# Gated units' projections as products of rounded high and low parts, with the convolution taps reordered around the gating

## The chip, the cores and the metric

The kernel runs on one core of one Trainium2 chip. The metric is the device time of one execution in microseconds (us). The engines are PE (TensorE: matmuls, with PEld, its weight loads, shown apart), DVE (VectorE), ACT (ScalarE), POOL (GpSimd) and SP (SyncE, which only issues transfers here). Each engine works through its own program in order and waits on semaphores.

## The reference, cut to what matters

One layer of a diffusion backbone works on 1024 latent tokens (a 16 x 64 grid) and 256 context tokens, with 1024 model columns. The part at issue is the first half of the combined projection and what is made of it:

```python
h = rms_norm(x, norm1_g) * (1 + scale1) + shift1
u = h @ w_in                                # 1024 -> 4608 columns
val, gate = u[..., :512], u[..., 512:1024]  # the convolution branch
v = val * sigmoid(gate)                     # the gated units
v = depthwise_conv(v, width=31) + dw_b      # per channel, over tokens
v = silu(layer_norm(v)) @ w_pw
q, k, value = three blocks of 512 columns of u, for the attention
```

Behind it come the neighbourhood attention, the merge of the two branches with its projections, the output projection, a router that picks tokens for 16 experts (SwiGLU, 1024 to 2048 to 1024), and a final RMSNorm. All data are float32, and the change leaves what is computed as it is, up to rounding.

## The kernel before, in words

**Layout.** Activations stand transposed: `hT` holds h as 8 chunks k of 128 channels (partitions) by 1280 tokens. The tokens are worked on in three blocks tc of 512, 512 and 256 (`TOK`). Almost all of SBUF is one float32 tensor `arena`; named regions of it are reused (HT, CONV, GLU, Q, K, V, R). The helpers `mm` (line 658) and `tr` (line 661) record all matmuls and transposes. A matmul whose operands are float32 stands in the trace as two records; one whose operands are of type fp32r (float32 rounded for the array) stands as one.

**Front.** The input rows are squared, scaled by 1/rms (DVE, ACT), transposed on PE, and copied into `hT`. PE also makes the first columns of the modulation vectors (`ada`, `ada_turn`). Then `affine` turns `hT` into h in place: even chunks on ACT (line 1225), odd chunks on DVE (line 1638).

**Gated units** (PE from line 714 with half = 0; ACT line 1235; DVE line 1672). Four units j = 2i + jj, each for 128 value columns and the 128 gate columns that belong to them. SP loads the weights of unit j into `ws[j % 2]` (lines 387 and 388) once unit j - 2 has been multiplied, and the modulation weights (line 393) for two `ada` calls per unit. For each unit and token block PE multiplies 2 banks x 8 chunks (bank `2*tc` the values, `2*tc+1` the gates), each as a plain float32 matmul. ACT takes the sigmoid of the gate bank, DVE multiplies it with the value bank into `glu` (`gated_unit`) and raises `u_free`, which lets PE reuse the two banks. Between them PE does `ada` behind blocks 0 and 1 and `ada_turn` behind blocks 1 and 2, and ACT copies their results (lines 1143 and 1147) right behind the sigmoid of its block; PE's next `ada_turn` waits for that copy.

**Convolution** (DVE, lines 1674 to 1711). For each of 4 channel groups, 31 taps over 1310 columns: tap 0 is a scale and bias (line 1679), the other 30 are multiply-adds `conv = glu * dw + conv` (line 1683), each waiting for the one before it. Their order against the gating is written out by hand: DVE gates a block, then does some taps, then gates the next one. Behind the last tap `conv_done` is raised.

**Queries and keys** (the same PE loop with half = 1). Four more passes of the same shape, plain float32 matmuls into the same banks. ACT empties both banks (lines 1242 and 1243), raises `qk_free`, and makes the modulation copies. Before the first pass PE waits once, for all the gating (`u_free` 15).

**Behind it.** PE sums over channels for the LayerNorm (`channel_sums`, waits for `conv_done`), then come values, attention, the merge, the output projection and the experts. The merge and the experts already multiply in three products: the high part of each operand is its fp32r rounding (ACT Copy), the low part is the rest (DVE subtract, line 1846 for h, 1800 for weights), and PE does high x high, high x low and low x high. GpSimd works in the front only on memsets; later it adds attention biases (lines 568 to 578), sums softmax terms, and issues the gathers (line 631) and scatters (lines 639 and 642) of the experts, which read their row numbers from SBUF.

## Time and profile before

| | |
|---|---|
| median of 3 executions | 2777.97 us (2774.75 to 2778.36) |
| the profiled execution | 2777.72 us, span 2775.9 us |
| PE busy | 2656.1 us, 96% of the span |
| DVE, ACT, POOL busy | 1725.9, 1284.0, 192.4 us |
| gated units on PE | 51.4 to about 204 us |
| queries and keys on PE | 205.0 to about 355 us |
| convolution on DVE | 91.9 to 294.8 us |
| attention, merge, output projection, experts | the rest |

The span runs from the first to the last instruction of the core; the time of the execution is 1.8 us longer. All times in the rows are from the span's start. A mean of "one" is the duration of one record; records of matmuls overlap, so the rate of PE is read from where successive weight loads start. "Idle" names the time an engine stood still before an instruction and what ended it.

### The profile page before, as it was taken

Reading aid. Unit: us, or ns where it says so; the run is one execution under the profiler, and the core shown is the slowest. Engines: PE = TensorE matmul, PEld = TensorE weight load, DVE = VectorE, ACT = ScalarE, POOL = GpSimd, SP = SyncE. Lnnn points to the kernel's source line nnn. Section 1 sums busy time; section 2 is a strip of 40 time slices with the busy share of each in tenths; the row PEclk is TensorE's granted clock in tenths of the full one; section 3 lists DMA queues with packets and bytes.
Section 4 is the critical chain, followed back from the end, with each engine's and each line's share of the span. In section 5 each row is a group of like instructions: output and inputs, shape, how many; then the busy total and the mean of one; then the engine's idle time right before and its main releaser. Section 6 shows DMA issues by size and latency. Waiting matters only on the chain.

```text
span 2775.9 us, 49590 instructions
## 1 busy us (share of the span) xinstructions
PE 2656.1 (96%) x21723; PEld 2024.0 (73%) x21723; DVE 1725.9 (62%) x2079; ACT 1284.0 (46%) x1867; POOL 192.4 (7%) x180
## 2 busy tenths in 40 slices
PE   6999999999999999869999999999999999999994
PEld 3555577666777897647887788778777877787783
DVE  4699234766434354556676677767667676776664
ACT  4000034555323232255565556656565555555554
POOL 0000011110000000000110011001101110110000
PEclk9999999999999999979999999999999999999997
DMA  8322222000333372277898889789879888898884
GB/s 260 91 90 78 61 56 50 15 1 25 91 100 98 99 202 110 107 243 268 283 298 258 283 291 287 268 281 293 281 265 298 276 282 274 288 296 259 283 276 169
DMA packets 457504, 543.75 MB, mean 196 GB/s; under 512 B 26304, under 2 KB 409387, under 8 KB 457290
## 3 DMA queue, kind: packets, MB, share of 16 engines
q1 hardware_dynamic: 449610, 519.60, 57.2%
q0 software_dynamic: 7680, 20.98, 3.4%
q8 instruction: 173, 2.83, 0.4%
q14 instruction: 41, 0.34, 0.0%
HBM read 513.27 MB, written 27.28 MB: 195 GB/s over the span
## 4 chain that ended last, share of the span: by engine, by line
PE 90%; DVE 5%; ACT 2%; DMA 1%; issue 1%; SPq 0%; POOL 0%; DVEq 0%; POOLq 0%; ACTq 0%
PE bank L658 85%; PE bank L661 4%; DVE arena L1683 2%; DVE arena L1756 1%; DVE arena L1766 1%; ACT arena L1287 1%; DVE arena L2102 0%; DMA arena<-in_x_sample 0%; ACT arena L1291 0%; DMA arena<-xhat,arena 0%; DMA arena<-in_w_attn_o 0%; DMA arena<-in_w_in 0%; DVE arena L1612 0%; DMA yacc<-arena 0%; DMA arena<-yacc 0%
## 5 line engine op out<-in xcount | busy, mean ns | idle before, releaser
L2032 DVE TENSOR_TENSOR slot_lo<-slot,e_hi 128x2048 fp32r<-128x2048 f32 x256 | 579.4, 2289 | 166.3 <-ACT e_hi L1496 162.6
L658 PE MATMUL bank<-arena 128*64 128x128 f32 (+8 forms) x3492 | 636.1, 396 | 19.0 <-ACT arena L1287 5.1
L658 PEld LDWEIGHTS bank<-arena 128*128 128x128 f32 (+3 forms) x3492 | 388.8, 163 | 238.5 <-issue 170.9
L1496 ACT ACTIVATE e_hi<-slot 128x2048 fp32r<-128x2048 f32 x256 | 481.4, 1917 | 0.0
L658 PE MATMUL bank<-e_hi,xe_hi 128*128 128x512 f32 x1024 | 418.0, 408 | 0.0
L658 PE MATMUL bank<-e_hi,xe_lo 128*128 128x512 f32 x1024 | 404.7, 395 | 0.0
L658 PE MATMUL bank<-slot_lo,xe_hi 128*128 128x512 f32 x1024 | 400.2, 391 | 0.0
L658 PE MATMUL bank<-slot,arena 128*32 128x128 f32 (+1 forms) x10240 | 363.6, 297 | 6.1 <-DVE arena L2042 3.5
L658 PEld LDWEIGHTS bank<-slot,arena 128*32 128x32 f32 x10240 | 285.2, 111 | 72.6 <-issue 34.2
L2036 DVE TENSOR_TENSOR slot_lo<-slot,e_hi 128x2048 fp32r<-128x2048 f32 x128 | 289.0, 2291 | 77.8 <-ACT e_hi L1498 77.8
L661 PE MATMUL bank<-arena 128*128 128x128 f32 (+3 forms) x1415 | 202.6, 275 | 54.9 <-DVE arena L1612 12.3
L1498 ACT ACTIVATE e_hi<-slot 128x2048 fp32r<-128x2048 f32 x128 | 239.4, 1912 | 29.6 <-PE bank L658 29.6
L661 PEld LDWEIGHTS bank<-arena 128*128 128x128 f32 (+3 forms) x1415 | 161.5, 142 | 114.2 <-issue 77.1
L658 PEld LDWEIGHTS bank<-e_hi,xe_hi 128*128 128x128 f32 x1024 | 191.9, 187 | 58.8 <-issue 16.1
L658 PEld LDWEIGHTS bank<-slot_lo,xe_hi 128*128 128x128 f32 x1024 | 192.4, 188 | 47.5
L658 PEld LDWEIGHTS bank<-e_hi,xe_lo 128*128 128x128 f32 x1024 | 192.5, 188 | 37.0
L1518 ACT ACTIVATE arena<-bank 128x256 f32<-128x256 f32 x128 | 49.2, 385 | 359.8 <-PE bank L658 359.8
L658 PE MATMUL bank<-e_hi,hT_hi 128*128 128x512 f32 x512 | 209.4, 409 | 0.0
L658 PE MATMUL bank<-e_hi,hT_lo 128*128 128x512 f32 x512 | 202.3, 395 | 0.0
L658 PE MATMUL bank<-slot_lo,hT_hi 128*128 128x512 f32 x512 | 200.0, 391 | 0.0
L1683 DVE SCALAR_TENSOR_TENSOR arena<-arena 128x1310 f32<-128x1310 f32 x120 | 189.9, 1583 | 4.0
L1800 DVE TENSOR_TENSOR w_down<-arena,w_up 128x2048 fp32r<-128x2048 f32 x23 | 52.7, 2293 | 141.5 <-ACT wx_up L1341 95.9
(231 smaller groups left out, 2878.8 us busy)
## 6 DMA issues: line engine op xcount, KB each, us to landing
slot<-in_w_gate_e SPq DMA_DIRECT2D x128, 1024.0 KB, 5.9
slot<-in_w_up_e SPq DMA_DIRECT2D x128, 1024.0 KB, 9.2
slot<-in_w_down_e SPq DMA_DIRECT2D x128, 1024.0 KB, 6.7
arena<-in_w_in SPq DMA_DIRECT2D x68, 512.0 KB, 5.1
arena<-in_w_ada SPq DMA_DIRECT2D x48, 512.0 KB, 4.8
arena<-in_w_conv_pw SPq DMA_DIRECT2D x24, 256.0 KB, 5.6
arena<-in_w_attn_o SPq DMA_DIRECT2D x24, 256.0 KB, 5.3
yacc<-arena SPq DMA_DIRECT2D x10, 512.0 KB, 2.6
```

What stands on the lines that cost most here:

```text
L658: return nc.tensor.matmul(out, lhsT, rhs, start=start, stop=stop)
L661: return nc.tensor.transpose(out, in_, ident[0:n, 0:n])
L1287: A_(Pctx[g % 2][h][:, 0:n], bank[3 + h][:, 0:n], ACT.Exp, bias=m, accum_out=sums[:, g % 2, h, 1:2]).then_inc(pc_ok, 1)
L1496: A_(halves(e_hi[c % 2])[:, :, rows4, :], halves(slot[q])[:, :, rows4, :], ACT.Copy).then_inc(ehi_ok, 1)
L1498: A_(e_hi[c % 2][:, 8 * h:8 * h + 8, :], slot[q][:, 8 * h:8 * h + 8, :], ACT.Copy).then_inc(ehi_ok, 1)
L1518: A_(sil[:, (c - 1) % 2, :], bank[(c - 1) % 2][:, 0:256], ACT.Silu).then_inc(silu_ok, 1)
L1683: V_.scalar_tensor_tensor(out=conv[:, k, :], in0=glu[:, k, t:t + CONV_W], scalar=dw[:, k, t:t + 1], in1=conv[:, k, :], op0=ALU.mult, op1=A ...
L1756: V_.tensor_reduce(mx[:, g % 2, h, 1:2], bank[3 + h][:, 0:n], AX_X, ALU.max).then_inc(c_max, 1)
L1766: V_.tensor_copy(PT[:, h, o:o + 512], src).then_inc(tg_dve, 1)
L1800: last = V_.tensor_tensor(dst, src[:, 0:16, :], w_up[s].bitcast(F32), ALU.subtract)
L2032: V_.tensor_tensor(halves(slot_lo[q])[:, :, rows4, :], halves(slot[q])[:, :, rows4, :], halves(e_hi[c % 2])[:, :, rows4, :].bitcast(F32), ...
L2036: V_.tensor_tensor(slot_lo[q][:, rows8, :], slot[q][:, rows8, :], e_hi[c % 2][:, rows8, :].bitcast(F32), ALU.subtract).then_inc(elo_ok, 1)
```

## The change

Four things are changed. First, the gated units' matmuls become three fp32r products each: high and low parts of h (`g_up`, `g_down`) and of the unit's weights (`gw_up`, `gw_down`). ACT rounds the high parts (24 pieces of h and 8 half weights); DVE subtracts the low parts of h (24) and of the first unit's weights (2), and GpSimd those of the other three units' weights (6). `g_down` lies where `hT` lies and `gw_down` where `ws` lies, so the plain values are overwritten; `g_up` lies in the regions K and V and `gw_up` in Q, where queries and keys are written later. Second, GpSimd adds the parts of h back into `hT` (24 adds), each block as soon as the last gated unit has multiplied it; PE's first queries wait for each chunk (`pool_sum`), and ACT waits for all 24 before it writes the first query. Third, the one wait for all gating before the queries becomes a wait per token block. Fourth, the taps are dealt out anew. `res9` becomes `pool_sum`, and waits on shared semaphores further on get offsets.

```diff
--- before.py
+++ after.py
@@ -151,6 +151,10 @@
         w_down_first = rounded_at("w_down_first", K, 16, P)
         h_up = [rounded_at(f"h_up{q}", GLU + 1024 * q, 2, 512) for q in range(KD // 2)]
         h_down = [rounded_at(f"h_down{q}", HT + 2 * T * q, 2, T) for q in range(KD // 2)]
+        g_up = [rounded_at(f"g_up{c}", K + T * c, 1, T) for c in range(KD)]
+        g_down = [h_down[c // 2][:, c % 2, :] for c in range(KD)]
+        gw_up = [rounded_at(f"gw_up{i}", Q + 2048 * i, KD, 256) for i in range(2)]
+        gw_down = [rounded_at(f"gw_down{i}", R + 2048 * i, KD, 256) for i in range(2)]
         wo = plain_at("wo_raw", HT, KD, T)[:, :, 0:D]
         wo_conv = rounded_at("wo_conv", CONV, KC, CONV_W)[:, :, 0:D]
         wo_attn = rounded_at("wo_attn", Q, KC, T)[:, :, 0:D]
...
@@ -560,6 +564,19 @@
             nc.gpsimd.memset(eps_zero[0:1, :], 0.0).then_inc(rpb_zero, 1)
             nc.gpsimd.memset(wr, 0.0)
             nc.gpsimd.memset(glu, 0.0).then_inc(pads, 1)
+
+            pool.wait_ge(wl_ok, 2)
+            for j in range(1, 4):
+                for half in range(2):
+                    pool.wait_ge(wh_ok, 2 * j + half + 1)
+                    ks = slice(4 * half, 4 * half + 4)
+                    nc.gpsimd.tensor_tensor(gw_down[j % 2][:, ks, :], ws[j % 2][:, ks, :], gw_up[j % 2][:, ks, :].bitcast(F32),
+                                            ALU.subtract).then_inc(wl_ok, 1)
+            for tc, (t0, n) in enumerate(TOK):
+                pool.wait_ge(u_ready, 18 + 2 * tc + 2)
+                for c in range(KD):
+                    nc.gpsimd.tensor_tensor(hT[:, c, t0:t0 + n], g_up[c][:, 0, t0:t0 + n].bitcast(F32),
+                                            g_down[c][:, t0:t0 + n].bitcast(F32), ALU.add).then_inc(pool_sum, 1)
             pool.wait_ge(conv_done, 1)
             def bias_rows(hp, h):
...
@@ -712,19 +729,29 @@
             for half in range(2):
-                if half:
-                    pe.wait_ge(u_free, 15)
                 for i in range(0, 2):
                     for jj in range(2):
+                        j = 2 * i + jj
                         pe.wait_ge(ws_in[jj], i * 32 + (64 + 64 * half))
                         for tc, (t0, n) in enumerate(TOK):
+                            if half and j == 0:
+                                pe.wait_ge(u_free, 12 + tc + 1)
                             pe.wait_ge(qk_free if half else u_free, i * 6 + (3 * jj + tc + 1))
                             for h in range(2):
+                                out, cols = bank[2 * tc + h][:, 0:n], slice(P * h, P * h + P)
                                 for k in range(KD):
-                                    if half == i == jj == h == 0:
-                                        pe.wait_ge(h_dve if k % 2 else h_act, 4 * tc + k // 2 + 1)
-                                    last = mm(bank[2 * tc + h][:, 0:n], ws[jj][:, k, P * h:P * h + P], hT[:, k, t0:t0 + n],
-                                              k == 0, k == KD - 1)
+                                    if half:
+                                        if j == h == 0:
+                                            pe.wait_ge(pool_sum, 8 * tc + k + 1)
+                                        last = mm(out, ws[jj][:, k, cols], hT[:, k, t0:t0 + n], k == 0, k == KD - 1)
+                                    else:
+                                        if tc == h == 0 and k % 4 == 0:
+                                            pe.wait_ge(wl_ok, 2 * j + k // 4 + 1)
+                                        if j == h == 0:
+                                            pe.wait_ge(hl_ok, 8 * tc + k + 1)
+                                        mm(out, gw_up[jj][:, k, cols], g_up[k][:, 0, t0:t0 + n], k == 0, False)
+                                        mm(out, gw_up[jj][:, k, cols], g_down[k][:, t0:t0 + n], False, False)
+                                        last = mm(out, gw_down[jj][:, k, cols], g_up[k][:, 0, t0:t0 + n], False, k == KD - 1)
                                 last.then_inc(u_ready, 1)
                             if tc:
                                 ada_turn(5 + tc, i * 4 + (8 * half + 2 * jj + tc + 8))
...
@@ -906,8 +933,8 @@
-                        pe.wait_ge(wl_ok, i * 2 + (8 * tc + s + 1))
-                        pe.wait_ge(hl_ok, 12 * tc + 4)
+                        pe.wait_ge(wl_ok, 8 + i * 2 + (8 * tc + s + 1))
+                        pe.wait_ge(hl_ok, 24 + 12 * tc + 4)
...
@@ -1216,14 +1243,44 @@
                         A_(dst[:, c, t0:t0 + n], bank[4 + g % 4][:, 0:n], ACT.Identity, bias=Bc[:, c, cnd:cnd + 1],
                            scale=Ac[:, c, cnd:cnd + 1]).then_inc(done, 1)
             act.wait_ge(t1_act, 12)
-            for g, (c, tc) in enumerate(tile_groups()):
-                if g % 2 == 0:
-                    t0, n = TOK[tc]
-                    cnd = 1 if tc == 2 else 0
-                    if tc == 0:
-                        act.wait_ge(mod1_ok, c // 4 + 1)
-                    A_(hT[:, c, t0:t0 + n], hT[:, c, t0:t0 + n], ACT.Identity, bias=sh1[:, c, cnd:cnd + 1],
-                       scale=A1[:, c, cnd:cnd + 1]).then_inc(h_act, 1)
+            def affine(tc, c):
+
+                t0, n = TOK[tc]
+                cnd = 1 if tc == 2 else 0
+                if tc == 0:
+                    act.wait_ge(mod1_ok, c // 4 + 1)
+                A_(hT[:, c, t0:t0 + n], hT[:, c, t0:t0 + n], ACT.Identity, bias=sh1[:, c, cnd:cnd + 1],
+                   scale=A1[:, c, cnd:cnd + 1]).then_inc(h_act, 1)
+
+            def g_hi(tc, cs_):
+
+                t0, n = TOK[tc]
+                for c in cs_:
+                    act.wait_ge(h_dve if c % 2 else h_act, 4 * tc + c // 2 + 1)
+                    A_(g_up[c][:, 0, t0:t0 + n], hT[:, c, t0:t0 + n], ACT.Copy).then_inc(hh_ok, 1)
+
+            def gw_hi(j, half):
+
+                act.wait_ge(ws_in[j % 2], 64 + 32 * (j // 2))
+                ks = slice(4 * half, 4 * half + 4)
+                A_(gw_up[j % 2][:, ks, :], ws[j % 2][:, ks, :], ACT.Copy).then_inc(wh_ok, 1)
+
+            act.wait_ge(t1_ready, 24)
+            affine(0, 0)
+            affine(0, 2)
+            g_hi(0, range(0, 4))
+            gw_hi(0, 0)
+            affine(0, 4)
+            affine(0, 6)
+            g_hi(0, (4, 5))
+            gw_hi(0, 1)
+            g_hi(0, (6, 7))
+            for tc in (1, 2):
+                for c in range(0, KD, 2):
+                    affine(tc, c)
+                g_hi(tc, range(KD))
+            gw_hi(1, 0)
+            gw_hi(1, 1)
             for i in range(0, 2):
...
@@ -1234,6 +1291,10 @@
                         act.wait_ge(u_free, i * 6 + (m + 2))
                         A_(sg[:, m % 2, 0:n], bank[2 * tc + 1][:, 0:n], ACT.Sigmoid).then_inc(sg_ok, 1)
                         ada_steps(tc, i * 4 + (2 * jj + 8), i * 8 + (16 + 4 * jj))
+                        if tc == 0 and 1 <= 2 * i + jj <= 2:
+                            for part in range(2):
+                                gw_hi(2 * i + jj + 1, part)
+            act.wait_ge(pool_sum, 24)
             for i in range(0, 2):
                 for jj in range(2):
                     for tc, (t0, n) in enumerate(TOK):
...
@@ -1648,8 +1709,28 @@
             link(V_.scalar_tensor_tensor(out=A1[:, 4:8, :], in0=sc1[:, 4:8, :], scalar=1.0, in1=bcast(CV["n1"] + 4, 4), op0=ALU.add, op1=ALU.mult))
             V_.memset(marks[:, 11:12], 0.0).then_inc(mod1_ok, 1)
             affine(0, (5, 7))
-            affine(1, (1, 3, 5, 7))
-            affine(2, (1, 3, 5, 7))
+
+            def g_lo(tc, cs_):
+
+                t0, n = TOK[tc]
+                for c in cs_:
+                    dve.wait_ge(hh_ok, 8 * tc + c + 1)
+                    V_.tensor_tensor(g_down[c][:, t0:t0 + n], hT[:, c, t0:t0 + n], g_up[c][:, 0, t0:t0 + n].bitcast(F32),
+                                     ALU.subtract).then_inc(hl_ok, 1)
+
+            def gw_lo(half):
+
+                dve.wait_ge(wh_ok, half + 1)
+                ks = slice(4 * half, 4 * half + 4)
+                V_.tensor_tensor(gw_down[0][:, ks, :], ws[0][:, ks, :], gw_up[0][:, ks, :].bitcast(F32), ALU.subtract).then_inc(wl_ok, 1)
+            g_lo(0, range(0, 4))
+            gw_lo(0)
+            g_lo(0, (4, 5))
+            gw_lo(1)
+            g_lo(0, (6, 7))
+            for tc in (1, 2):
+                affine(tc, (1, 3, 5, 7))
+                g_lo(tc, range(KD))
             def leave(dst, tc_, Ac, Bc, ready, done):
...
@@ -1685,27 +1766,27 @@
                     steps[0] += 1
             for tc in range(3):
                 gated_unit(0, tc)
-            taps(0, 0, 10)
+            taps(0, 0, 6)
             gated_unit(1, 0)
-            taps(0, 10, 18)
+            taps(0, 6, 14)
             gated_unit(1, 1)
-            taps(0, 18, 24)
+            taps(0, 14, 18)
             gated_unit(1, 2)
-            taps(0, 24, TAPS)
-            taps(1, 0, 1)
+            taps(0, 18, 26)
             gated_unit(2, 0)
-            taps(1, 1, 9)
+            taps(0, 26, TAPS)
+            taps(1, 0, 3)
             gated_unit(2, 1)
-            taps(1, 9, 14)
+            taps(1, 3, 7)
             gated_unit(2, 2)
-            taps(1, 14, 24)
+            taps(1, 7, 15)
             gated_unit(3, 0)
-            taps(1, 24, TAPS)
-            taps(2, 0, 1)
+            taps(1, 15, 23)
             gated_unit(3, 1)
-            taps(2, 1, 6)
+            taps(1, 23, 27)
             gated_unit(3, 2)
-            taps(2, 6, TAPS)
+            taps(1, 27, TAPS)
+            taps(2, 0, TAPS)
             taps(3, 0, TAPS)
             dve.wait_ge(chain, steps[0])
             V_.memset(marks[:, 4:5], 0.0).then_inc(conv_done, 1)
...
```

The cut leaves out the renamed semaphore and further offsets of the same kind in waits of the merge.

## Rows read from the trace of the kernel before

**Rows 1.** The page: busy times, shares of the chain that ended last, the taps

```profile
PE 2656.1 (96%) x21723; PEld 2024.0 (73%) x21723; DVE 1725.9 (62%) x2079; ACT 1284.0 (46%) x1867; POOL 192.4 (7%) x180
...
PE 90%; DVE 5%; ACT 2%; DMA 1%; issue 1%; SPq 0%; POOL 0%; DVEq 0%; POOLq 0%; ACTq 0%
...
L1683 DVE SCALAR_TENSOR_TENSOR arena<-arena 128x1310 f32<-128x1310 f32 x120 | 189.9, 1583 | 4.0
```

**Rows 2.** Windows, first 38.6 us of the gated units: PE, PEld, DVE, ACT, POOL busy, clock, DMA share, GB/s

```profile
51.40:90.00 38.60, 38.56 (x129) 19.67 (x130) 3.17 (x8) 8.16 (x15) 0.00 (x0) 0.94 0.41 124
```

**Rows 3.** Timeline, start of the gated units: start, us, engine, line, operation, idle before

```profile
48.52 7.72 ACT L1225 ACTIVATE arena<-arena 128x512 f32<-128x512 f32 x12
...
51.44 2.07 PE L658 MATMUL bank<-arena 128*128 128x512 f32 x2 [3.02 <-DMA arena<-in_w_in]
```

**Rows 4.** Timeline of ACT: sigmoids of gate banks, the three blocks of unit 1

```profile
105.22 0.60 ACT L1235 ACTIVATE arena<-bank 128x512 f32<-128x512 f32 x1 [13.67 <-PE bank L658]
...
120.16 0.60 ACT L1235 ACTIVATE arena<-bank 128x512 f32<-128x512 f32 x1 [13.52 <-PE bank L658]
...
128.60 0.39 ACT L1235 ACTIVATE arena<-bank 128x256 f32<-128x256 f32 x1 [6.69 <-PE bank L658]
```

**Rows 5.** Timeline of PEld: plain and rounded matmuls, 512 and 256 columns

```profile
64.04 0.19 PEld L658 LDWEIGHTS bank<-arena 128*128 128x128 f32 x1 [0.24 <-issue]
64.47 0.19 PEld L658 LDWEIGHTS bank<-arena 128*128 128x128 f32 x1 [0.24 <-issue]
...
705.96 0.19 PEld L658 LDWEIGHTS bank<-h_up,w_up 128*128 128x128 f32 x1
...
706.64 0.19 PEld L658 LDWEIGHTS bank<-h_up,w_up 128*128 128x128 f32 x1
...
963.15 3.44 PEld L658 LDWEIGHTS bank<-arena 128*128 128x128 f32 x16
...
985.43 0.19 PEld L658 LDWEIGHTS bank<-h_up,w_up 128*128 128x128 f32 x1
...
985.78 0.19 PEld L658 LDWEIGHTS bank<-h_up,w_up 128*128 128x128 f32 x1
```

**Rows 6.** Timeline: DVE's taps and idle time; PE's start of the queries

```profile
68.37 0.69 DVE L1672 TENSOR_TENSOR arena<-bank,arena 128x512 f32<-128x512 f32 x1 [15.18 <-ACT arena L1235]
...
107.98 12.91 DVE L1683 SCALAR_TENSOR_TENSOR arena<-arena 128x1310 f32<-128x1310 f32 x8
...
205.03 2.41 PE L658 MATMUL bank<-arena 128*128 128x512 f32 x5 [1.02 <-DVE arena L1672]
...
294.84 0.06 DVE L1711 MEMSET arena<- 128x1 f32 x1
359.63 2.49 DVE L1718 SCALAR_TENSOR_TENSOR arena<-bank,arena 128x512 f32<-128x512 f32 x4 [64.73 <-PE bank L658]
```

**Rows 7.** Groups by line, shapes apart: busy us, mean ns | idle before

```profile
L1846 DVE TENSOR_TENSOR h_down<-arena,h_up 128x1024 fp32r<-128x1024 f32 x8 | 9.3, 1220 | 6.8 <-ACT h_up L1376 6.8
L1349 ACT ACTIVATE a_up<-arena 128x512 fp32r<-128x512 f32 x16 | 8.6, 619 | 0.0
L1376 ACT ACTIVATE h_up<-arena 128x1024 fp32r<-128x1024 f32 x8 | 7.8, 1046 | 8.2 <-PE bank L658 8.2
L568 POOL TENSOR_TENSOR arena<-arena 128x896 f32<-128x896 f32 x8 | 16.7, 2090 | 367.4 <-DMA arena<-rpbp 367.3 <-issue 0.2
L593 POOL TENSOR_TENSOR arena<-arena 128x2 f32<-128x2 f32 x32 | 6.3, 197 | 210.1 <-issue 136.5 <-ACT arena L1291 73.6
L577 POOL TENSOR_TENSOR arena<-arena 128x512 f32<-128x512 f32 x4 | 5.1, 1270 | 0.0
```

**Rows 8.** Timeline: a scatter of POOL beside DVE, and one alone

```profile
1423.19 2.27 DVE L2032 TENSOR_TENSOR slot_lo<-slot,e_hi 128x2048 fp32r<-128x2048 f32 x1
1423.99 2.94 POOL L639 DMA_INDIRECT yacc<-arena  x1 [81.14 <-DVE arena L2083]
...
2740.68 1.55 POOL L639 DMA_INDIRECT yacc<-arena  x1 [81.86 <-DVE arena L2083]
```

More of the change, by code:

```diff
@@ L315, in backbone @@
         m_free, vv_ready, sum_ok, recip_ok, rinv_ok = (sem(n) for n in ("m_free", "vv_ready", "sum_ok", "recip_ok", "rinv_ok"))
-        rinv6, router, res9 = sem("rinv6"), sem("router"), sem("res9")
+        rinv6, router, pool_sum = sem("rinv6"), sem("router"), sem("pool_sum")
         HP = HEADS // 2
@@ L612, in _ @@
             pool.wait_ge(o6_done, 19)
-            nc.gpsimd.tensor_tensor(mt6[:, 0:2, :], mt6[:, 0:2, :], g1row[:, 4:6, :], ALU.mult).then_inc(res9, 1)
-            pool.wait_ge(res9, 1)
+            nc.gpsimd.tensor_tensor(mt6[:, 0:2, :], mt6[:, 0:2, :], g1row[:, 4:6, :], ALU.mult).then_inc(pool_sum, 1)
+            pool.wait_ge(pool_sum, 24 + 1)
             nc.gpsimd.tensor_tensor(x1[:, 9, 0:512].rearrange("p (a n) -> p a n", a=2), x1[:, 9, 0:512].rearrange("p (a n) -> p a n", a=2), mt6[:, 0:2, :], ALU.add).then_inc(x1_ok, 1)
             pool.wait_ge(o6_done, 20)
-            nc.gpsimd.tensor_tensor(mt6[:, 2:4, :], mt6[:, 2:4, :], g1row[:, 6:8, :], ALU.mult).then_inc(res9, 1)
-            pool.wait_ge(res9, 2)
+            nc.gpsimd.tensor_tensor(mt6[:, 2:4, :], mt6[:, 2:4, :], g1row[:, 6:8, :], ALU.mult).then_inc(pool_sum, 1)
+            pool.wait_ge(pool_sum, 24 + 2)
             nc.gpsimd.tensor_tensor(x1[:, 9, 512:1024].rearrange("p (a n) -> p a n", a=2), x1[:, 9, 512:1024].rearrange("p (a n) -> p a n", a=2), mt6[:, 2:4, :], ALU.add).then_inc(x1_ok, 1)
@@ L919, in _ @@
                         if not plain:
-                            pe.wait_ge(hl_ok, 12 * tc + 12)
+                            pe.wait_ge(hl_ok, 24 + 12 * tc + 12)
                             for q in range(KD):
@@ L1796, in weight_lo @@
             def weight_lo(s, tiles, both):
-                dve.wait_ge(wh_ok, tiles)
+                dve.wait_ge(wh_ok, 8 + tiles)
                 src, dst = (wm_first, w_down_first) if tiles == 1 else (wm[s], w_down[s])
@@ L1811, in a_lo @@
                 for m, q in enumerate(rows):
-                    dve.wait_ge(hh_ok, 12 * tc + 4 + m + 1)
+                    dve.wait_ge(hh_ok, 24 + 12 * tc + 4 + m + 1)
                     c0 = CONV_AT[tc] if q < KC else t0
@@ L1844, in h_lo @@
                 for q in range(KD // 2):
-                    dve.wait_ge(hh_ok, 12 * tc + q + 1)
+                    dve.wait_ge(hh_ok, 24 + 12 * tc + q + 1)
                     V_.tensor_tensor(h_down[q][:, :, t0:t0 + n], hT[:, 2 * q:2 * q + 2, t0:t0 + n],
```

## The prediction

> **What bounds the kernel now.** I read the page first: PE is busy for 2656.1 us, and 90% of the chain that ended last lies on PE [rows 1]. So a microsecond taken from PE counts, unless another engine then holds PE up. The window over the first 38.6 us of the gated units says the same: PE is busy in all of it but 0.04 us, while DVE works for 3.17 us, ACT for 8.16, and POOL never; transfers use 41% of the DMA engines [rows 2]. Then the timeline: DVE has ended the convolution at 294.84 and stands idle for 64.73 us until PE has finished the queries [rows 6]. The gated units and the queries are thus bound by PE, with room on the others.
>
> **Products, what they give back.** A plain matmul of 512 columns is two records, 0.43 us apart: 0.858 us. Three rounded products of the same size take 0.68 to 0.69 us (705.96 to 706.64, the same pair of operands one triple on); I take 0.688. With 256 columns, 8 plain matmuls (16 records) take 3.44 us, 0.43 each, and a triple 0.35 [rows 5]. A unit has 16 matmuls in each token block: 2 x 16 x (0.858 - 0.688) + 16 x (0.43 - 0.35) = 5.4 + 1.3 = 6.7 us. Four units: **-26.9 us**. A unit now takes 37.5 us (two blocks of unit 1 are 14.94 and 8.44 apart [rows 4], the third step 14.2), afterwards 12.2 + 7.15 + 11.45 = 30.8.
>
> **The start.** Now PE starts when the weights land, at 51.44 [rows 3]. Afterwards ACT, which begins its affines at 48.52 at 0.64 us each [rows 3], has done two of them and four roundings of h (0.54 to 0.62, [rows 7]) by about 52; then it rounds half of the weights (1.05 us for 1024 columns [rows 7], to 53), and DVE subtracts (1.22 us, [rows 7]). PE starts at 54.3: **+2.9 us**. The second half of the weights (ready about 57.9) is needed after four triples, and the low parts of h come each 0.6 us, faster than a triple. That first stretch runs partly at the low clock: 0.94 over 38.6 us is 2.3 us of work lost [rows 2], before and after alike. ACT's further 16 roundings, 8 affines and two half weights last until about 71; its first sigmoid comes at 72 in place of about 67, and PE needs the copy behind it only at 80. DVE's subtractions lie where it stood idle for 15.18 us [rows 6]. The rounding of units 2 and 3 (2 x 1.05 us each) goes behind a sigmoid, where ACT idles 13.5 us [rows 4]; POOL needs 2.4 us for each half then, and PE wants them some 18 us later. I cost these at nothing. No transfer is added or moved, and SP's queue is as it was.
>
> **The wait for gating.** PE now waits 1.02 us for the last gating before the queries [rows 6]; with a wait per block it goes: **-1.1 us**. If nothing else held PE up, the sum would be -26.9 + 2.9 - 1.1 = -25.1 us.
>
> **The taps.** A tap takes 1.61 us (12.91 for 8 [rows 6]). Between two gatings of the same block the new order has 20 taps: 32.3 + 1.5 for the gating = 33.8 us, against 30.8 for PE's unit. So DVE falls behind by some 3 us per unit. By its own work it gates block 0 of the last unit at 166.3: from 99.2 there are 39 taps at 1.615, one first tap (0.96) and 3.1 us of gatings. PE wants these banks at 179.7 (below). The lag alone costs nothing, and the convolution ends near 292, before PE's sums at 330.
>
> **GpSimd beside the taps.** This decides. POOL gets 6 weight halves and 24 adds, all with two inputs in SBUF, as each tap has. By its own rows an add of 512 columns takes 1.27 us and 896 columns 2.09, that is 2.1 ns per column: 2.36 for a half, 0.72 for 256 columns [rows 7]. No row shows such an operation beside a tap. The nearest do: a scatter on POOL takes 1.55 us when DVE idles, and 2.94 when a DVE subtract with two SBUF inputs is under way; that one ended at 1425.46 and the scatter 1.47 us later, its whole length [rows 8]. So POOL was held until DVE's instruction was over. The ends for one add beside taps are therefore 1.27 (no hindrance) and, each waiting for one whole tap of the other, 1.61 + 1.24 = 2.85; if the 0.2 us that a nearly empty POOL instruction takes (line 593, [rows 7]) overlaps the tap, 2.65. Nearest to rows 8 are the latter two, and I take 2.65 to 2.85, with the taps held by as much as POOL works. The Trainium skill says so too ("SBUF — State Buffer", section on the two separate sides): a VectorE instruction with two SBUF inputs and a GpSimd instruction that reads SBUF hold the shared ports for their whole length, one after the other. The trace agrees for one direction, POOL behind DVE; no row shows DVE behind POOL.
>
> Now in order of time, PE's last unit: block 0 ends at 54.3 + about 44.3 + 61.6 = 160.2, block 2 at 179.5. Four weight halves beside taps put DVE back by 4 x 2.36 = 9.4 us: gating of block 0 at 175.7. From 160.2 on each tap pairs with an add; some 9 of them, 1.24 each: 187. PE's first queries wait for it 7.4 us, then run 2.2 us longer at the low clock (as behind the stop at the start, [rows 2]). They end, with the ada behind them, at 204.2; the gating of block 1 comes 8 taps, 8 adds and itself later, about 210, wait 5.5, low clock 2.2. All adds are over by 223, when PE finishes that block, so ACT, which waits for all 24 and has behind this wait both the query copies and the modulation copy that PE's next turn needs, is just in time. Loss: 7.4 + 5.5 + 4.4 = 17.3. With 2.65 per add the waits are 5.0 and 4.6, and the loss 14.0. Net -25.1 + 14.0 to 17.3 = -11 to -8; forecast **-10 us**. The convolution then ends near 325, still before PE at about 345.
>
> **Against what.** The sum is made against the profiled execution: 2777.7 (span 2775.9 + 1.8), which is 0.25 us under the median. Forecast 2767.7, say 2768 us.
>
> **The rivals.**
> *Free (0.28).* POOL and the taps run side by side; a scatter makes descriptors, an add streams data, and may behave otherwise. Then adds of block 0 end at 170, block 1 at 182, all at 188, always ahead of PE: -25.1, **2752.6 us**. For it: DVE's subtracts in the experts keep their 2.27 to 2.3 us beside scatters [rows 8]. A form between lies here as well: POOL keeps the ports through its run of 8 adds, DVE stops 10 us at a time, and PE loses 0 to 8.
> *Starved (0.14), the slower side.* Place: the 24 adds after 160.2. If DVE takes the next tap before POOL gets in, an add passes two taps, 3.23 + 1.27 = 4.5 us. The adds end at 160.2 + 16 x 4.5 + 8 x 3.95 = 264; PE has then stood since 209 at its turn, which hangs on ACT behind the wait for all 24: 55 + 2.2 - 25.1 = +32, **2810 us**. It decides from about 3.2 us per 512-column add, where the adds end near 233. For it: the gap between two taps is only 0.03 us (1583 ns for one [rows 1], 1.61 from start to start). Against: the margin from 2.85 must be passed on average.
> *The products give less (0.03).* If triples ran at the plain rate, -26.9 would go and 17 us be lost: 2797. Rows 5 speak against it.
>
> **How the numbers follow.** Forecast 0.55, its own range 2762 to 2771; free 0.28; starved 0.14; weak products 0.03. A change of 0.2% is 5.6 us, about what a measurement of this kernel tells from none. Faster by more: 0.28 + 0.51 = 0.79; within: 0.06 (the upper end of the forecast, and a loss of 20 to 30 us); slower: 0.15. The range reaches from the free case, less 2 us for the durations, to 2775, where a little more waiting than worked out is held: 2750 to 2775.
>
> **What would show it.** Products: in the gated stretch weight loads 0.23 us apart, sigmoids of the same block 30.8 us apart. Start: first product at 54.3. Contention: taps of line 1683 with a mean well above 1583 ns, or gaps before them, and POOL adds above 1.27 us or 2.65 to 2.85 apart; PE idle for some 5 to 8 us before the first queries and again before the second block. Free: taps stay at 1583 ns, PE has no wait over 1 us there. Starved: adds over 3.2 us apart and a stop of PE on ACT. The forecast is wrong if PE's waits come elsewhere, above all at the first unit, or if the convolution ends after PE asks for it.

## The result and the profile after

The changed kernel takes **2761.07 us** (median of 5 runs, 2760.72 to 2762.97); the kernel before took 2775.53 us beside it (5 runs, 2774.75 to 2778.36). The ratio is 0.9945, 95% interval 0.9932 to 0.9959: 14.5 us faster, where 10 were forecast. The profiled execution after is the median run itself, 2761.07 us with a span of 2759.0.

The page after, the lines that answer to [rows 1] (L675 is the matmul, L578 GpSimd's adds of the two parts of h, L1764 the taps):

```profile
PE 2631.9 (95%) x21915; PEld 2046.7 (74%) x21915; DVE 1764.7 (64%) x2105; ACT 1302.1 (47%) x1899; POOL 268.0 (10%) x210
...
PE 89%; DVE 3%; POOL 2%; ACT 1%; SPq 1%; issue 1%; DMA 1%; DVEq 0%; POOLq 0%; ACTq 0%
...
L1764 DVE SCALAR_TENSOR_TENSOR arena<-arena 128x1310 f32<-128x1310 f32 x120 | 213.6, 1780 | 4.0
```

PE is busy 24 us less. The taps are as many as before and of the same shape, but their mean is 1780 ns in place of 1583, and POOL has a place of its own in the chain. Where, the timeline shows: L1292 is the sigmoid, L1303 a query copy, L1170 the modulation copy, L573 the subtraction of a weight half, L1753 a gating, L1792 the end of the convolution.

```profile
53.99 0.76 PE L675 MATMUL bank<-g_up,gw_up 128*128 128x512 f32 x1 [6.18 <-DVE gw_down L1725]
...
80.11 0.60 ACT L1292 ACTIVATE arena<-bank 128x512 f32<-128x512 f32 x1 [7.69 <-PE bank L675]
...
111.24 0.60 ACT L1292 ACTIVATE arena<-bank 128x512 f32<-128x512 f32 x1 [8.98 <-PE bank L675]
...
132.51 7.40 POOL L573 TENSOR_TENSOR gw_down<-arena,gw_up 128x1024 fp32r<-128x1024 f32 x2 [24.85 <-ACT gw_up L1266]
...
161.25 56.12 POOL L578 TENSOR_TENSOR arena<-g_up,h_down 128x512 f32<-128x512 f32 x24 [21.33 <-PE bank L675]
...
124.35 16.95 DVE L1764 SCALAR_TENSOR_TENSOR arena<-arena 128x1310 f32<-128x1310 f32 x8
...
161.19 19.28 DVE L1764 SCALAR_TENSOR_TENSOR arena<-arena 128x1310 f32<-128x1310 f32 x8
180.39 0.68 DVE L1753 TENSOR_TENSOR arena<-bank,arena 128x512 f32<-128x512 f32 x1
181.00 19.52 DVE L1764 SCALAR_TENSOR_TENSOR arena<-arena 128x1310 f32<-128x1310 f32 x8
200.44 0.68 DVE L1753 TENSOR_TENSOR arena<-bank,arena 128x512 f32<-128x512 f32 x1
...
181.17 14.97 PE L675 MATMUL bank<-arena 128*128 128x512 f32 x48
201.18 16.39 PE L675 MATMUL bank<-arena 128*128 128x512 f32 x32 [5.03 <-DVE arena L1753]
218.81 16.45 PE L675 MATMUL bank<-arena 128*128 128x2 f32 x73 [1.25 <-ACT arena L1170]
...
217.40 0.60 ACT L1303 ACTIVATE arena<-bank 128x512 f32<-128x512 f32 x1 [35.78 <-POOL arena L578]
...
316.13 0.06 DVE L1792 MEMSET arena<- 128x1 f32 x1
344.74 2.48 DVE L1799 SCALAR_TENSOR_TENSOR arena<-bank,arena 128x512 f32<-128x512 f32 x4 [28.55 <-PE bank L675]
```

Read from the top. PE starts the gated units at 53.99, 2.55 us later than [rows 3]. Sigmoids of the same block are 31.13 us apart, where a unit took 37.5: 6.4 us gained in each of four. PE reaches the queries at 181.17 (205.03 in [rows 6]), 23.9 us earlier; that is 4 x 6.4 - 2.55 and some 0.8 of the old 1.02 us wait. Then it stands 5.03 us for the gating of block 1, at 200.44, and 1.25 us for ACT, which had stood 35.78 us for GpSimd's last add. Eight taps that took 12.91 us [rows 6] take 16.95 beside two weight halves, 19.28 and 19.52 beside adds. The wait at DVE's next step behind the queries ends at 344.74, where [rows 6] has 359.63: 14.9 us earlier. So 9.0 of the 23.9 us are given back between 181 and 345.

The weight loads behind the 5 us stop show the part that no wait shows, and the windows (their columns as in [rows 2]) the clock:

```profile
201.17 0.50 PEld L675 LDWEIGHTS bank<-arena 128*128 128x128 f32 x2 [5.51 <-DVE arena L1753]
...
203.04 0.34 PEld L675 LDWEIGHTS bank<-arena 128*128 128x128 f32 x1 [0.52 <-issue]
203.90 0.34 PEld L675 LDWEIGHTS bank<-arena 128*128 128x128 f32 x1 [0.52 <-POOL arena L578]
...
206.24 0.19 PEld L675 LDWEIGHTS bank<-arena 128*128 128x128 f32 x1 [0.30 <-issue]
206.67 0.19 PEld L675 LDWEIGHTS bank<-arena 128*128 128x128 f32 x1 [0.24 <-issue]
```

```profile
60.00:160.00 100.00, 100.00 (x582) 81.67 (x581) 79.22 (x67) 22.84 (x48) 18.45 (x6) 1.00 0.32 95
...
201.00:209.00 8.00, 7.83 (x13) 3.51 (x14) 7.89 (x6) 0.00 (x0) 8.00 (x5) 0.69 0.00 1
209.00:217.00 8.00, 8.00 (x20) 3.43 (x19) 7.89 (x6) 0.00 (x0) 8.00 (x5) 1.00 0.00 0
```

From 201.17 to 206.24 loads are 0.86 us apart instead of 0.43: PE works at the lower of its two clocks (1.2 of 2.4 GHz; the mean granted from 201 to 209 is 0.69) for 5.1 us and loses 2.5. 5.0 + 1.3 + 2.5 = 8.8, which is the 9.0 but for 0.2. The 2 us by which the two profiled spans (2775.9 and 2759.0) differ beyond the 14.9 lie behind the queries, where nothing was changed; the kernel before varies by 3.6 us from run to run.

### The profile page after: what moved, and what is told of

Its sections match the earlier page's. It is cut to its first block, busy times and chain, and to the rows that moved or that the text cites. A ratio compares the mean times of both kernels' runs of the same rounds, so it can differ in the third digit from the quotient of the medians.

```text
span 2759.0 us, 50069 instructions
## 1 busy us (share of the span) xinstructions
PE 2631.9 (95%) x21915; PEld 2046.7 (74%) x21915; DVE 1764.7 (64%) x2105; ACT 1302.1 (47%) x1899; POOL 268.0 (10%) x210
## 3 DMA queue, kind: packets, MB, share of 16 engines
q8 instruction: 174, 2.85, 0.4%
## 4 chain that ended last, share of the span: by engine, by line
PE 89%; DVE 3%; POOL 2%; ACT 1%; SPq 1%; issue 1%; DMA 1%; DVEq 0%; POOLq 0%; ACTq 0%
PE bank L675 85%; PE bank L678 4%; POOL arena L578 2%; SPq L397 1%; DVE arena L1837 1%; DVE arena L1847 1%; ACT arena L1348 1%; DVE arena L2183 0%; DMA arena<-in_w_ada 0%; ACT arena L1352 0%; DMA arena<-xhat,arena 0%; DVE arena L1844 0%; DMA yacc<-arena 0%; DMA arena<-yacc 0%; DVE slot_lo L2113 0%
## 5 line engine op out<-in xcount | busy, mean ns | idle before, releaser
L675 PE MATMUL bank<-arena 128*64 128x128 f32 (+8 forms) x3108 | 498.2, 381 | 20.8 <-ACT arena L1348 5.1
L675 PEld LDWEIGHTS bank<-arena 128*64 128x64 f32 (+3 forms) x3108 | 316.5, 160 | 173.4 <-issue 104.4
L675 PE MATMUL bank<-e_hi,xe_hi 128*128 128x512 f32 x1024 | 418.1, 408 | 0.0
L675 PE MATMUL bank<-e_hi,xe_lo 128*128 128x512 f32 x1024 | 404.7, 395 | 0.0
L675 PE MATMUL bank<-slot_lo,xe_hi 128*128 128x512 f32 x1024 | 400.2, 391 | 0.0
L675 PE MATMUL bank<-slot,arena 128*32 128x128 f32 (+1 forms) x10240 | 363.5, 297 | 6.0 <-DVE arena L2123 3.5
L675 PEld LDWEIGHTS bank<-slot,arena 128*32 128x32 f32 x10240 | 285.2, 111 | 72.5 <-issue 34.0
L678 PEld LDWEIGHTS bank<-arena 128*128 128x128 f32 (+3 forms) x1415 | 161.8, 142 | 114.0 <-issue 77.3
L675 PEld LDWEIGHTS bank<-e_hi,xe_hi 128*128 128x128 f32 x1024 | 191.9, 187 | 58.8 <-issue 16.1
L675 PEld LDWEIGHTS bank<-slot_lo,xe_hi 128*128 128x128 f32 x1024 | 192.3, 188 | 47.5
L675 PEld LDWEIGHTS bank<-e_hi,xe_lo 128*128 128x128 f32 x1024 | 192.5, 188 | 37.0
L1764 DVE SCALAR_TENSOR_TENSOR arena<-arena 128x1310 f32<-128x1310 f32 x120 | 213.6, 1780 | 4.0
L675 PE MATMUL bank<-e_hi,hT_hi 128*128 128x512 f32 x512 | 209.4, 409 | 0.0
L675 PE MATMUL bank<-e_hi,hT_lo 128*128 128x512 f32 x512 | 202.3, 395 | 0.0
L675 PE MATMUL bank<-slot_lo,hT_hi 128*128 128x512 f32 x512 | 200.0, 391 | 0.0
L656 POOL DMA_INDIRECT yacc<-arena x16 | 45.7, 2859 | 1314.0 <-DVE arena L2164 1314.0
```

Source lines behind the costliest of these rows:

```text
L656: nc.gpsimd.indirect_dma_start(out=yacc, out_offset=bass.IndirectOffsetOnAxis(ap=sidx[:, 0:1].bitcast(U32), axis=0), in_=ye, in_offset=Non ...
L675: return nc.tensor.matmul(out, lhsT, rhs, start=start, stop=stop)
L678: return nc.tensor.transpose(out, in_, ident[0:n, 0:n])
L1764: V_.scalar_tensor_tensor(out=conv[:, k, :], in0=glu[:, k, t:t + CONV_W], scalar=dw[:, k, t:t + 1], in1=conv[:, k, :], op0=ALU.mult, op1=A ...
```

## The experiments

The theory was that of the forecast: GpSimd's instruction and a tap, each with two inputs in SBUF, take turns at ports that only one can hold; that stretches the taps, makes gatings late and costs PE about 9 us. Against it stood three other readings: that the adds cost because they stand between PE's units and its queries, wherever they run; that the order of the taps, 20 in a unit, is too much by itself; and that any GpSimd instruction costs DVE something, whatever it reads. The kernel before took 2777.74 us beside the first four runs (15 runs, 2775.41 to 2780.89) and 2779.2 beside the others (14 runs, 2776.93 to 2781.65); across the two, ratios are compared. A second measure leaves out what varies behind the queries: the start of DVE's next step behind them, 359.63 in the kernel before and 344.74 in the changed one. It is called the mark below.

**1. dve_adds: the 24 adds on DVE.** Eight stand behind each gating of the last unit; GpSimd's are gone.

```diff
-                    nc.gpsimd.tensor_tensor(hT[:, c, t0:t0 + n], g_up[c]..., g_down[c]..., ALU.add).then_inc(pool_sum, 1)
+            def add_back(tc):
+                dve.wait_ge(u_ready, 18 + 2 * tc + 2)
+                for c in range(KD):
+                    V_.tensor_tensor(hT[:, c, t0:t0 + n], g_up[c]..., g_down[c]..., ALU.add).then_inc(pool_sum, 1)
             gated_unit(3, 0)
+            add_back(0)
             taps(1, 15, 23)
```

> The 24 adds that put h back are moved from GpSimd to DVE, 8 behind each gating of the last unit. Ports theory (a tap and a GpSimd add hold each other up, which costs PE about 10 us in its waits at 195 to 219): the taps go back to 1583 ns wherever GpSimd is idle, DVE spends 16 x 0.61 + 8 x 0.36 = 12.6 us on the adds in place of some 20 us of stretched taps, PE's waits of 5.5 us and 2.1 us and the low clock behind them go, and the time falls by 8 to 10 us against the changed kernel, to about 2752. Rival (DVE's load alone holds PE up, since DVE has more to do than PE in the last units): DVE has 12.6 us more of its own work before the last gatings, the wait stays or grows, and the time stays within 2 us of the changed kernel or rises.

Measured: 2754.75 us (5 runs, 2752.86 to 2758.28), ratio 0.9914 [0.9901, 0.9928], an interval that lies below that of the changed kernel. Timeline of DVE (L1759 taps, L1748 gatings, L1767 the adds):

```profile
161.50 12.91 DVE L1759 SCALAR_TENSOR_TENSOR arena<-arena 128x1310 f32<-128x1310 f32 x8
174.32 0.69 DVE L1748 TENSOR_TENSOR arena<-bank,arena 128x512 f32<-128x512 f32 x1
174.92 4.90 DVE L1767 TENSOR_TENSOR arena<-g_up,h_down 128x512 f32<-128x512 f32 x8
179.74 12.91 DVE L1759 SCALAR_TENSOR_TENSOR arena<-arena 128x1310 f32<-128x1310 f32 x8
192.56 0.68 DVE L1748 TENSOR_TENSOR arena<-bank,arena 128x512 f32<-128x512 f32 x1
```

An add costs DVE 0.60 us of its own (4.82 from the first of eight to the next tap). Eight on GpSimd make eight taps 6.4 us longer (19.28 less 12.91), which is 0.80 for each. The gating of block 1 is there at 192.56 (over at 193.24, and PE asks at about 195.7), and PE waits for nothing over 0.5 us; the adds end at 207.4 instead of 217.4. The mark comes at 335.77, 9.0 us before the changed kernel's, as expected (8 to 10). So the place of the adds is not what costs: the same adds in the same place cost PE nothing.

**2. adds_copy: a copy in place of each add.** GpSimd copies the high part of h alone, so that queries, keys and values are made of h without its low part.

```diff
-                    nc.gpsimd.tensor_tensor(hT[...], g_up[c]..., g_down[c]..., ALU.add).then_inc(pool_sum, 1)
+                    nc.gpsimd.tensor_copy(hT[...], g_up[c]...).then_inc(pool_sum, 1)
```

> GpSimd copies the high part into h's place in place of adding the two parts: one SBUF input. Left out: the low part of h for queries, keys and values. Ports theory as I stated it (GpSimd reading SBUF at all is what collides with a tap of two inputs): taps beside a copy stay stretched, by 0.4 to 0.9 us each, and the copy, well under 1.27 us alone, takes over 1.6 us. Rival (only two-input GpSimd instructions collide, since the second stream is what is shared): taps at 1583 ns beside the copies, PE's wait at 195 gone, time about 2751.

Measured: 2754.01 us (one run). Groups by form, then the timeline (L578 the copies, L1763 the taps):

```profile
L578 POOL COPY arena<-g_up 128x512 f32<-128x512 f32 x16 | 28.4, 1826 | 21.3 <-PE bank L674 21.3
```

```profile
161.22 37.61 POOL L578 COPY arena<-g_up 128x512 f32<-128x512 f32 x24 [21.31 <-PE bank L674]
...
161.18 14.51 DVE L1763 SCALAR_TENSOR_TENSOR arena<-arena 128x1310 f32<-128x1310 f32 x8
```

A copy takes 1.83 us beside taps, a tap and a little more, but 0.61 where one fell beside a gating, which has one input in PSUM. The first line is that copy, the second the taps that were held (shortest, median and longest in ns):

```profile
L578 POOL COPY arena<-g_up x1: 612/612/612, 176.1 to 176.1; 128x512 f32<-128x512 f32 x1
L1763 DVE SCALAR_TENSOR_TENSOR arena<-arena x7: 1810/1811/1815, 162.8 to 173.9; 128x1310 f32<-128x1310 f32 x7
```

One input on GpSimd's side is thus enough for a copy to wait for a tap. It then holds the next tap up by 0.23 us (1.81 less 1.58), less than the 0.4 to 0.9 that were expected and a quarter of what an add does. PE waits for nothing over 0.5 us. The mark comes at 335.45, 9.3 us before the changed kernel's.

**3. adds_memset: a fill in place of each add.** No input at all; h is left out of queries, keys and values.

```diff
-                    nc.gpsimd.tensor_tensor(hT[...], g_up[c]..., g_down[c]..., ALU.add).then_inc(pool_sum, 1)
+                    nc.gpsimd.memset(hT[...], 0.5).then_inc(pool_sum, 1)
```

> GpSimd fills h's place with a constant in place of adding: no SBUF input. Left out: h for queries, keys and values. Ports theory: a write alone does not hold a tap up; taps at 1583 ns, the 24 fills over within 15 us, no wait of PE over 1 us at 181 to 219, time 8 to 10 us under the changed kernel, about 2752: this is what the change would give with the adds free. Rival (the waits come of the order of the taps and gatings, not of the adds): the gating of block 1 still comes after 195 and PE's wait stays above 3 us.

Measured: 2753.31 us (4 runs, 2752.24 to 2754.78), ratio 0.991 [0.9895, 0.9925].

```profile
160.64 3.80 POOL L578 MEMSET arena<- 128x512 f32 x8 [21.30 <-PE bank L674]
...
160.59 12.91 DVE L1763 SCALAR_TENSOR_TENSOR arena<-arena 128x1310 f32<-128x1310 f32 x8
```

Eight fills in 3.80 us, eight taps beside them in 12.91 as if GpSimd were idle; the mark comes at 334.88. PE waits for nothing over 0.5 us, so the new order of the taps is not too much by itself either. And it is not any instruction of GpSimd that costs; what counts is whether it reads. The Trainium skill ("SBUF — State Buffer", section on the two separate sides) names just this pair, a VectorE instruction with two SBUF inputs against a GpSimd one that reads SBUF, and the three runs agree.

**4. whole_wait: one wait for all gatings again.**

```diff
-                            if half and j == 0:
-                                pe.wait_ge(u_free, 12 + tc + 1)
+                            if half and j == tc == 0:
+                                pe.wait_ge(u_free, 15)
```

> The wait of PE's first queries is again for all gating at once (as before the change), all else as changed. With the gating of block 2 at 209 and PE ready at 181, PE stands for 28 us and then works at the low clock for a few us: the first two query blocks end near 240 in place of 219, and the time is 20 to 23 us above the changed kernel, about 2782, above the kernel before. Rival (waits per block buy only the 1 us that the wait cost before): 1 to 2 us above the changed kernel.

Measured: 2784.97 us (10 runs, 2781.24 to 2787.61), ratio 1.0024 [1.0014, 1.0033]: slower than the kernel before, and 0.8%, 22 us, slower than the changed one.

```profile
209.18 35.99 PE L675 MATMUL bank<-arena 128*128 128x512 f32 x118 [28.29 <-issue]
```

PE stands 28.29 us in one piece, until the last gating (at 208.84 in the changed kernel). Behind the stop the weight loads are 0.86 us apart from 209.15 to 212.63 only, and the clock granted from 209 to 217 is 0.78, so 1.7 us are lost to it. That makes 30.0, less the 9.0 of the changed kernel 21.0; the mark (365.41) comes 20.7 later. 20 to 23 were expected. In the forecast the wait per block stood at -1.1 us, the wait that it removes from the kernel before; it is the part without which the other parts lose everything, since with the adds on GpSimd DVE is 28 us behind PE once products are fast.

**5. split_adds: the same adds as 48 halves.** The test of whether a turn is paid per instruction: the data are the same, the instructions twice as many.

```diff
-                    nc.gpsimd.tensor_tensor(hT[:, c, t0:t0 + n], ...).then_inc(pool_sum, 1)
+                    for a in (t0, t0 + n // 2):
+                        last = nc.gpsimd.tensor_tensor(hT[:, c, a:a + n // 2], ...)
+                        last.then_inc(pool_sum, 1)
```

> Each of GpSimd's 24 adds is cut into two of half the columns: the same data, 48 instructions. If the two engines take turns instruction by instruction, each half add waits for one whole tap (1.61 us) and holds the next by a little: a 512-column add then costs about 2 x 1.8 = 3.6 us in place of 2.43, a 256-column one about 3.4, and all adds end near 161 + 16 x 3.6 + 8 x 3.4 = 246. The modulation copy behind them lets PE go on only then, so PE's stop on ACT is about 25 us and the time 25 to 30 us above the changed kernel, near 2788: slower than before the change. Rival (the two share the ports by volume, and a turn costs nothing by itself): the adds end at 217 to 225 as now, and the time is within 5 us of the changed kernel.

Measured: 2796.97 us (4 runs, 2794.9 to 2797.68), ratio 1.006 [1.0044, 1.0076]. Timeline, then PE's waits (us in total, times, longest):

```profile
160.81 86.95 POOL L579 TENSOR_TENSOR arena<-g_up,h_down 128x256 f32<-128x256 f32 x48 [21.32 <-PE bank L677]
...
160.76 15.42 DVE L1766 SCALAR_TENSOR_TENSOR arena<-arena 128x1310 f32<-128x1310 f32 x8
...
249.21 21.22 PE L677 MATMUL bank<-arena 128*128 128x2 f32 x77 [18.41 <-ACT arena L1172]
```

```profile
PE bank L677 <- ACT arena L1172: 18.4, 1, 18.4
PE bank L677 <- POOL arena L579: 13.2, 7, 2.8
```

An instruction of half the size takes 1.81 us all the same (86.95 / 48, in 32 of 256 columns and 16 of 128), the 1.61 of one tap and 0.2; for GpSimd the price is first of all a tap per instruction, and only then the columns. DVE is not held up more but less: eight taps take 15.42 us instead of 19.28, and the gating of block 0 comes at 176.10 instead of 180.39. What costs is the end of the adds. They last 87 us instead of 56, now hold the queries themselves up seven times, and then ACT and with it PE. Against the changed kernel the loss is 32 us by the ratios and 33.5 by the mark (378.20), more than the 25 to 30 expected: the stop on ACT is 18.4 us and not 25, but the seven waits of 13.2 were not foreseen. Here the mechanism of the rival Starved is seen, at its place, though by the number of instructions and not by a turn that passes two taps.

**6. old_taps: the old order of the taps, the rest as changed.**

```diff
-            taps(0, 0, 6)
+            taps(0, 0, 10)
             gated_unit(1, 0)
...
-            taps(1, 7, 15)
+            taps(1, 14, 24)
             gated_unit(3, 0)
-            taps(1, 15, 23)
+            taps(1, 24, TAPS)
+            taps(2, 0, 1)
             gated_unit(3, 1)
```

> The taps are dealt out against the gatings as before the change (24 to 26 per unit in place of 20), all else as changed. If the order matters: DVE has 24 x 1.61 + 1.5 = 40 us of work per unit against PE's 31.1, falls behind by 9 us per unit, gatings come late, banks and the modulation copies behind the sigmoids hold PE up in the gated units, and the time is 15 to 25 us above the changed kernel, near 2780. Rival (the slack of a whole unit in the banks covers it): within 3 us of the changed kernel.

Measured: 2775.8 us (10 runs, 2772.86 to 2778.49), ratio 0.9986 [0.9977, 0.9996]. Timeline:

```profile
173.51 24.83 DVE L1764 SCALAR_TENSOR_TENSOR arena<-arena 128x1310 f32<-128x1310 f32 x10
198.26 0.68 DVE L1753 TENSOR_TENSOR arena<-bank,arena 128x512 f32<-128x512 f32 x1
...
199.04 0.38 ACT L1292 ACTIVATE arena<-bank 128x256 f32<-128x256 f32 x1 [24.42 <-DVE arena L1753]
...
199.04 41.51 PE L675 MATMUL bank<-arena 128*128 128x512 f32 x139 [18.81 <-issue]
```

Ten taps beside adds (2.48 each) stand ahead of the gating of block 0, which comes at 198.26 in place of 180.39; ACT's last sigmoid waits for it too, and PE stands 18.8 us once. The new order is worth 0.41%, some 11 us, of a gain of 14.5 (the mark, at 356.04, comes 11.3 later). That is less than the 15 to 25 expected, and it does not come as expected: PE is never held up in the gated units themselves, only once, before the queries. What the order is worth with the adds on DVE was not tried.

**7. dve_all: the weight subtractions on DVE as well.** GpSimd does nothing beside the taps.

```diff
+            def weight_rest(j):
+                for half in range(2):
+                    dve.wait_ge(wh_ok, 2 * j + half + 1)
+                    V_.tensor_tensor(gw_down[j % 2]..., ws[j % 2]..., gw_up[j % 2]..., ALU.subtract).then_inc(wl_ok, 1)
-            taps(0, 6, 14)
+            taps(0, 6, 9)
+            weight_rest(2)
+            taps(0, 9, 14)
```

> On top of the adds on DVE, the six subtractions for the weights of the other units go to DVE too; GpSimd then does nothing beside the taps. Ports theory: the four halves held the taps for 2.03 us each, DVE needs 1.2 us for each itself, so DVE ends the convolution about 1 us sooner (two more halves, 2.4 us, lie where it was idle), every tap takes 1583 ns, and PE, which did not wait for DVE any more, gains nothing: within 1.5 us of the version with the adds on DVE. Rival (the halves held back PE as well): 3 us or more below it.

Measured: 2753.21 us (5 runs, 2751.86 to 2754.9), ratio 0.9904 [0.989, 0.9918]; the convolution ends at 309.0. DVE ends 3.75 us sooner than in dve_adds (312.75), where about 1 was expected: four halves held taps for 2.03 each and cost DVE some 1.2 of its own. PE gains nothing by it: the mark comes at 335.84, where dve_adds has 335.77. It has the lowest median of this study, though its interval overlaps that of dve_adds, so moving the six subtractions adds nothing that can be told. Both beat the kernel before and the changed one.

**8. probe: the price of each kind, by itself.** Behind the 24 adds, beside the last taps, GpSimd does 8 adds, 8 copies and 8 fills of 512 columns on a tile that is not yet in use.

```diff
+            for n in range(8):
+                nc.gpsimd.tensor_tensor(vtok[:, 2 + n, :], vtok[:, 0, :], vtok[:, 1, :], ALU.add).then_inc(pool_sum, 1)
+            pool.wait_ge(pool_sum, 33)
+            for n in range(8):
+                nc.gpsimd.tensor_copy(vtok[:, 2 + n, :], vtok[:, 0, :]).then_inc(pool_sum, 1)
+            pool.wait_ge(pool_sum, 41)
+            for n in range(8):
+                nc.gpsimd.memset(vtok[:, 2 + n, :], 0.0).then_inc(pool_sum, 1)
```

> As changed, and behind its adds GpSimd does 8 additions (two SBUF inputs), 8 copies (one) and 8 fills (none), each 512 columns, beside the taps of the last groups, where PE waits for neither. Ports theory: additions 2.4 to 2.5 us each with taps stretched to about 2.4 us; copies about 1.6 to 1.9 us with taps stretched by about 0.2 us; fills 0.5 us with taps at 1583 ns. PE's waits and the time are as in the changed kernel, within 2 us. Rival (what stretches both is the fp32r reading or the sharing of h's region, not the ports): the plain additions take 1.27 us and the taps 1583 ns.

Measured: 2763.25 us (one run).

```profile
218.72 19.33 POOL L585 TENSOR_TENSOR arena<-arena 128x512 f32<-128x512 f32 x8
238.11 14.71 POOL L588 COPY arena<-arena 128x512 f32<-128x512 f32 x8
252.89 3.79 POOL L591 MEMSET arena<- 128x512 f32 x8
...
217.78 57.46 DVE L1777 SCALAR_TENSOR_TENSOR arena<-arena 128x1310 f32<-128x1310 f32 x30
```

2.42, 1.84 and 0.47 us each, in one kernel, at one place, against the same taps. Thirty taps take 57.46 us; alone they take 48.54 (at 218.10 in the changed kernel). Eight taps held by 0.89 and eight by 0.23 (medians of 2.47 and 1.81 us less 1.58) make 9.0, the 8.9 but for rounding. So it is neither the fp32r operands nor h's region that matters. PE's long wait is that of the changed kernel (5.0 us; the one on ACT is 1.9 instead of 1.25) and the mark comes at 344.43, since all of this lies behind: the taps' lag alone costs nothing, only a gating behind it does.

## Why the forecast was right, and by how much not

The direction and the mechanism were right. Of the two stops forecast before query blocks only the second came, and the size of one term, the loss to GpSimd beside the taps, was wrong: 14.0 to 17.3 us forecast, 9.0 measured. Point by point:

**Products, -26.9.** Right, 5% too large: a unit takes 31.13 us, not 30.8, so -25.6. The difference is 0.33 us in 48 triples. Within a block the loads are 0.231 us apart (46 steps from 162.20 to 172.83), so a triple of 512 columns takes 0.693 us and not 0.688, which is half of it; the rest lies in the triples of 256 columns and between the blocks and was not taken apart.

**The start, +2.9.** +2.55 (53.99, not 54.3).

**The wait for gating, -1.1.** PE starts the queries without a stop of more than 0.2 us: about -0.8. But the forecast priced the wait per block only by the wait that it removes. whole_wait shows that it carries 21 to 22 us.

**The weight halves.** Costed as holding DVE up by their own length, 2.36 us each. They do so by 2.03 (16.95 less 12.91, in two): 8.1 us for four, not 9.4.

**The pair of tap and add: this is the step that failed.** "The latter two, and I take 2.65 to 2.85, with the taps held by as much as POOL works." The first line below has the taps between the start of the adds and the gating of block 0 that were held up, the second those beside weight halves, the third those beside 256-column halves in split_adds (shortest, median and longest in ns):

```profile
L1764 DVE SCALAR_TENSOR_TENSOR arena<-arena x7: 2483/2496/2502, 162.8 to 178.0; 128x1310 f32<-128x1310 f32 x7
L1764 DVE SCALAR_TENSOR_TENSOR arena<-arena x2: 3605/3606/3606, 134.1 to 137.7; 128x1310 f32<-128x1310 f32 x2
L1766 DVE SCALAR_TENSOR_TENSOR arena<-arena x7: 1935/1942/1948, 162.4 to 174.2; 128x1310 f32<-128x1310 f32 x7
```

A held tap takes 2.50 us, so it is held 0.91, though the add takes 1.27 alone [rows 7], and a pair takes 2.53 from one tap to the next. Some 0.35 us of an add runs beside the tap; I had allowed for 0.2 at most. The forecast also let some 9 taps be held before the gating of block 0. There were eight, and the first of them had started before the first add, so seven were. Seven at 0.91 are 6.4 us, where nine at 1.04 to 1.24 were 9.4 to 11.2; the weight halves take off another 1.3. The gating of block 0 comes at 180.39 and not at 185 to 187, just ahead of PE (181.17), so that the first stop of 5.0 to 7.4 us, and the low clock behind it, are not there. The gating of block 1 comes at 200.44, and PE waits 5.03 us, as forecast (4.6 to 5.5) but 9 us earlier. That this wait has the forecast size is luck: DVE needs 20.0 us from one gating to the next and not 22 to 23, but PE, without the low clock, also needs 2.2 us less for its block. The forecast's 14.0 to 17.3 us of loss are 9.0.

**"ACT just in time".** Off by 1.25 us. The adds end at 217.4, before the 223 of the forecast, but PE comes sooner by the stop that fell away.

**The low clock.** 2.5 us behind one stop of 5 us, 2.2 forecast behind each of two. Behind the stop of 1.25 us there is none (granted clock 1.00 from 218.8 to 224).

**The convolution** ends at 316.1, not 325, and 28.6 us before DVE's next step. Right that it costs nothing.

The sum with measured terms: -25.6 + 2.55 - 0.8 + 9.0 = -14.9, as the timeline has it behind the queries; -14.5 by the medians.

**The rivals.** Free is refuted by the taps' 1780 ns in the changed kernel and shown as a state in adds_memset and dve_adds: 2753 to 2755 us, where 2752.6 was worked out for it. Starved did not come about: the longest of the 24 adds took 2673 ns and of the 48 halves 2116, so none passed two taps, although DVE leaves only 0.03 us between taps. Weak products are refuted by the first 100 us.

The Trainium skill (same page and section) has whoever holds the shared ports keep them for the whole instruction, the other blocked fully. By that the pair would take 1.58 + 1.27 = 2.85 us. The runs agree that each holds the other up, in both directions, and disagree on the length: 2.53. What part of GpSimd's instruction runs beside the tap (its start, its end) no run here separates.

## What to carry to other kernels

Before handing work to an idle GpSimd, look at what the vector engine does meanwhile: beside instructions with two inputs in SBUF each of GpSimd's that reads SBUF makes both wait, and here doing the add on the busy engine (0.60 us) was cheaper for that engine than having it done next door (0.80 on average). If it must be GpSimd, ask which end is waited for: few large instructions bring GpSimd's own end forward, small ones (split_adds) put it far back but hold the vector engine up less. A wait that is worth 1 us today may be worth 20 once the engine behind it gets faster, so price it against the kernel as it will be.

## What the runs showed of the hardware that was not expected

- A GpSimd instruction that reads SBUF waits for one tap of a back-to-back stream, however small it is: with the 1.61 us of the tap, an add of 512 columns comes every 2.53 us (1.27 alone) and the 48 halves of 256 and 128 every 1.81 on average. Each of the two subtractions of 1024 columns at 132.51 takes 3.7 (2.38 at 69.44, where no tap runs).
- What it takes from the tap behind it is its own length alone less 0.35 to 0.4 us: 2.02 for 1024 columns, 0.91 for 512, 0.23 for a copy of 512 (0.61 alone). For an add of 256 columns it is 0.36. The gatings, which have one input in PSUM, are not held up (0.68 us with an add under way, 0.69 without).
- Two inputs on DVE's side are not needed for it. The first tap of a group, a scale and bias with one input in SBUF, took 1.36 us beside an add (so too in whole_wait, split_adds, old_taps and probe) and 0.96 elsewhere:

```profile
L1760 DVE TENSOR_SCALAR arena<-arena x4: 954/961/1364, 88.2 to 266.6; 128x1310 f32<-128x1310 f32 x4
```

- A fill is untouched and touches nothing (0.47 us, taps at 12.91 for eight).
- The time that PE spends at the low clock behind a stop did not grow with the stop: 5.1 us behind one of 5.0, 5.1 behind 18.8 (old_taps, 199.01 to 204.12), 3.5 behind 28.3 (whole_wait), and none behind 1.25.
